# Output and query projections of tiles 1 to 3: low halves one piece ahead, rows behind them, eight more gathered rows

## What is computed

```python
h = rms_norm(x, norm_mix)
q, k, v, u_g, v_g = split(h @ w_in)              # 2048 x 5120
y = concat(rms_norm(stick_breaking(q, k, v)), rms_norm(gmlp(u_g, v_g)))
x = x + y @ w_out                                # the output projection
h2 = rms_norm(x, norm_ffn)
# product-key retrieval, 8 heads x 16 experts of 16384 for each token
s = rms_norm(h2 @ peer_w_query) . sub_keys       # the query projection
idx, gate = top16(s)
act = gelu(einsum('tkd,td->tk', peer_u[idx], h2)) * gate
x = x + einsum('tk,tkd->td', act, peer_v[idx])
```

## Time and profile before

| | us |
|---|---|
| median of 3 runs | 2888.29 |
| lowest and highest | 2881.99, 2889.8 |
| the profiled execution | 2884.2 |
| its span, first to last instruction | 2882.5 |

### The profile page before, as it was taken

The page is one execution under the profiler, slowest core; times in us unless marked ns, Lnnn a source line. Parts: engine busy times, 40 slices in busy tenths (PEclk is TensorE's granted clock), DMA queues, the critical chain, the costliest instruction groups (busy, mean ns, idle before and its releaser), DMA issues.

```text
span 2882.5 us, 43296 instructions
## 1 busy us (share of the span) xinstructions
PE 2769.8 (96%) x17757; PEld 2612.8 (91%) x17757; DVE 2156.8 (75%) x2920; ACT 1256.1 (44%) x1692; POOL 1485.8 (52%) x657
## 2 busy tenths in 40 slices
PE   8899999988999999999999999998999999999998
PEld 6687778866788999999999999998999999999998
DVE  6856897767587778889997677776676777777786
ACT  7656632347424333337775333333333333333332
POOL 0100253322232348872223788887867776767762
PEclk9999999999999999999999999999999999999999
DMA  9747678974697969998999999999999999999996
GB/s 362 297 154 273 242 265 344 341 268 156 252 347 289 359 255 338 339 347 346 361 363 372 379 367 382 375 373 336 359 370 358 385 363 378 377 384 361 384 344 229
DMA packets 188846, 949.47 MB, mean 329 GB/s; under 512 B 17712, under 2 KB 77152, under 8 KB 78912
## 3 DMA queue, kind: packets, MB, share of 16 engines
q1 hardware_dynamic: 116064, 485.54, 45.1%
q0 software_dynamic: 60848, 440.59, 39.2%
q10 hardware_dynamic: 11808, 21.70, 2.1%
HBM read 906.46 MB, written 41.22 MB: 329 GB/s over the span
## 4 chain that ended last, share of the span: by engine, by line
PE 73%; DMA 9%; DVE 9%; ACT 5%; POOL 2%; issue 2%; SPq 0%; ACTq 0%; DVEq 0%; POOLq 0%
PE ps L1847 9%; PE ps L2147 9%; PE ps L2145 9%; PE ps L2146 9%; PE ps L2214 8%; PE ps L2216 8%; PE ps L2215 8%; PE ps L2130 5%; PE ps L1834 3%; DVE ring_lo L1188 3%; DMA rows<-peer_u_rows,idx_far 2%; PE ps L2188 2%; DMA g_in<-gelu_scratch 2%; POOL ring_lo L658 2%; DVE rows L1461 2%; ACT ring_hi L744 2%
## 5 line engine op out<-in xcount | busy, mean ns | idle before, releaser
L658 POOL TENSOR_TENSOR ring_lo<-ring_raw,ring_hi 128x2048 fp32r<-128x2048 f32 x203 | 942.2, 4642 | 527.7 <-ACT ring_hi L744 525.6
L744 ACT ACTIVATE ring_hi<-ring_raw 128x2048 fp32r<-128x2048 f32 x396 | 754.7, 1917 | 664.8 <-DMA ring_raw<-peer_u 233.5
L2214 PE MATMUL ps<-a_hi,ring_hi 128*128 128x304 f32 x2048 | 624.0, 305 | 19.9 <-POOL ring_lo L658 13.8
L2145 PE MATMUL ps<-bT_hi,ring_hi 128*128 128x304 f32 x2048 | 622.7, 304 | 9.8 <-POOL ring_lo L658 8.3
L2216 PE MATMUL ps<-a_hi,ring_lo 128*128 128x304 f32 x2048 | 620.0, 303 | 0.0
L2147 PE MATMUL ps<-bT_hi,ring_lo 128*128 128x304 f32 x2048 | 617.8, 302 | 0.0
L2215 PE MATMUL ps<-a_lo,ring_hi 128*128 128x304 f32 x2048 | 617.0, 301 | 0.0
L2146 PE MATMUL ps<-bT_lo,ring_hi 128*128 128x304 f32 x2048 | 615.7, 301 | 0.0
L1188 DVE TENSOR_TENSOR ring_lo<-ring_raw,ring_hi 128x2048 fp32r<-128x2048 f32 x197 | 460.6, 2355 | 129.8 <-ACT ring_hi L744 129.5
L695 POOL DMA_INDIRECT rows<-peer_u_rows,idx_far x128 | 206.0, 1609 | 452.8 <-DVE z_far L1461 398.0
L2214 PEld LDWEIGHTS ps<-a_hi,ring_hi 128*128 128x128 f32 x2048 | 386.2, 189 | 25.2 <-issue 17.9
(11 more groups left out here) (328 smaller groups left out, 3759.8 us busy)
## 6 DMA issues: line engine op xcount, KB each, us to landing
ring_raw<-peer_u SPq DMA_DIRECT2D x128, 1024.0 KB
ring_raw<-peer_v SPq DMA_DIRECT2D x128, 1024.0 KB
ring_raw<-w_in SPq DMA_DIRECT2D x80, 1024.0 KB
ring_raw<-w_out SPq DMA_DIRECT2D x32, 1024.0 KB
ring_raw<-w_query SPq DMA_DIRECT2D x32, 1024.0 KB
g_quad<-gates_scratch SPq DMA_DIRECT2D x32, 640.0 KB
gelu_scratch<-ahead ACTq DMA_DIRECT2D x72, 152.0 KB
g_in<-gelu_scratch SPq DMA_DIRECT2D x72, 152.0 KB
```

The source lines that it names most:

```text
L658: pool.tensor_tensor(ring_lo[s][:], ring_raw[s][:], ring_hi[s][:].bitcast(F32), ALU.subtract)\
L744: act.activation(ring_hi[place(n)][:], ring_raw[place(n)][:], ACT.Copy).then_inc(hi_ok[SLOT[n]], 1)
L2145: pe.matmul(dst, hi[:, e], bT_hi[:, k, 0:NEAR], start=(k == 0), stop=False)
L2214: pe.matmul(dst, hi[:, col], a_hi[:, par, e, :], start=(e == 0), stop=False)
```

## The change

In the output projection VectorE no longer goes to the low half of piece n+2 before the rows of piece n; it stays at n+1. In the query projection it goes to n+1 instead of n+2. The rows of n follow behind. `ROWS_AT` is changed there: in the output projection the pieces with n % 4 == 3 (115, 119, 123) get two rows instead of one (piece 126 keeps one, 127 none); in the query projection n = 128, 131, 134, 137 and 140 get three instead of two (142 and 143 keep none). That is 62 rows instead of 54 in the two stages. Pieces 144 to 283 keep their counts, with the rows' indices shifted by eight, and pieces 284 to 395 share 139 rows instead of 147.

```diff
@@ -147,7 +147,7 @@
     for n in range(OUT_B, AHEAD - 1):
-        ROWS_AT[n] = 0 if n == QUERY_B - 1 else 1 if n == QUERY_B - 2 or n % 4 == 3 and n < QUERY_B else 2
+        ROWS_AT[n] = 0 if n == QUERY_B - 1 else 1 if n == QUERY_B - 2 else 3 if n >= QUERY_B and n % 3 == 2 else 2
     ROWS_AT[AHEAD - 2] = 0
@@ -1594,7 +1594,6 @@
                     for t in range(TB):
                         add_x1((n - OUT_B) // 4 - 1, t)
-                lo_upto(min(n + 2, QUERY_B))
                 rows_step(ROWS_AT[n])
@@ -1614,7 +1613,7 @@
                 if n > QUERY_B and n % 4 == 0:
                     add_squares((n - QUERY_B) // 4 - 1)
-                lo_upto(min(n + 2, AHEAD - 1))
+                lo_upto(min(n + 1, AHEAD - 1))
                 if n == QUERY_B + 1:
```

## The result

The changed kernel takes 2897.16 us (median, 2879.16 to 2913.27), the kernel before in the same comparison 2881.89 (2873.72 to 2893.0): ratio 1.006, 95% interval 1.0045 to 1.0075. It is slower by 0.6%; I had forecast 2885.3 us and no difference. The profiled execution is 2907.5 us long (span 2905.8), 10 us above its median; before's was 2884.2, so this pair of profiles shows more than the medians do (23.3 against 15.3 us).

What follows compares the result with a forecast made beforehand. TensorE, busy 2769.8 of 2882.5 us, was taken to bound the kernel. Terms -3.0 + 0 + 1.2 - 1.2 + 0 made -3.0 us, from the 2888.3 us median to 2885.3 us, range 2876 to 2897.

Steps and rivals of the forecast that it cites:

- What bounds the kernel: Whole kernel: TensorE busy 2769.8 of 2882.5 us; inside the two projections nothing to win, only to lose.
- The sign that I had named for a wrong Part 2 or 3: TensorE waiting more than 4 us for VectorE's low halves between 754 and 1043 us.
- Part 2: Output projection, three more rows: gathers at 8.5 us per buffer stay balanced, 0 us; +2 at 9.5, +4.5 at 10.
- Part 1: Output projection's tail: low halves one ahead free VectorE at 873.9 instead of 878.3 us; -3.0 us, bounds -3.1 and -0.7.
- Part 3: Query projection, low halves one ahead and five more rows: TensorE waits once, for low half 133, +1.2 us.
- (a): Rival: gathers become the limit in both projections, from 9.5 us per buffer on; 2901 us, chance 0.14.
- Part 4: Behind piece 284, eight rows fewer: a few late loads' idle time is won, -1.2 us, bounds -8.9 and +3.
- The store stall: GpSimd's wait storing the first tile's result, then TensorE's 6.63 us: not removed, change 0, bounds -4 and +4.
- (b): Rival: late stalls vanish, the 8.9 us behind 2095 and the tail's 3.0; 2876 us, chance 0.14.
- The sum: All terms: -3.0 + 0 + 1.2 - 1.2 + 0 = -3.0 us, 2885.3 us on the median; chance 0.60.

Runs made afterwards that it cites:

- the experiment with this part alone: Kernel before with only the output projection's new order and three more rows, late doubled rows moved too; query projection as before: 2883.89 us, 1.0003.
- the changed kernel's second profile: The changed kernel, unedited, run again beside the one with all late doubled rows at pieces with (n-284) % 4 == 0: 2892.12 us, 1.0027 against the kernel before.
- the profile with all landings: Changed kernel with all 27 late doubled rows at pieces with (n-284) % 4 == 0, its second run: 2897.64 us, 1.0047 against the kernel before.
- This part alone: Kernel before with only the query projection's new order and five more rows, late doubled rows mostly at (n-284) % 4 == 0: 2892.20 us, 1.0047.
- doubles forced to phase 1: Kernel before, 28 of 35 late two-row pieces put at (n-284) % 4 == 1, ahead of VectorE's low half: 2939.91 us, 1.0204; second profiled execution 2924.76 us.

## Why the prediction was wrong

**What bounds the kernel** held: the two projections had nothing to give and something to lose. The sign that I had named for a wrong Part 2 or 3, over 4 us of waits for low halves between 754 and 1043, came: 10.1 us in four.

**Part 1 (-3.0)** was right in its mechanism and too small here. VectorE's first addition came at 877.76, not at 875: VectorE was free at 877.4 instead of 873.9, since rows had waited for gathers, and then it waited 0.33 us more for TensorE, which the stalls of Part 2 had made late. Of the three waits for diagonals one of 0.89 us is left. With the clock, which I had not counted in the tail, it is -5.1 us in both profiles of the changed kernel; kernels with the order alone show -0.2 to -5.1.

**Part 2 (0)** failed as well. It was mis-sized by the gather: I took 8.5 us per buffer, and in this stage the median gather is 10.0 to 10.2 us plus 0.3. At 10 us my own count gives +4.5. TensorE stalled 3.67 us and the sixteen pieces took 6.7 us more, 3.0 of it not counted as waits, at least in part the lower clock behind a stall; in the changed kernel's second profile they took 4.0 us more. The larger gain of Part 1 hid this: together the output projection ended at +0.2 us in the profile, and the experiment with this part alone measured 1.0003. The DMA rate came out at 361 GB/s, as worked out (362), so the bytes were not the error; the time of one gather among them was. The Trainium skill (DMA: Bandwidth & Descriptors, Anatomy of one DMA, SWDGE path) gave 4.4 us by my estimate; no gather of the chain in these two stages is under 8.4, and the shortest of the profile with all landings is 6.5.

**Part 3 (+1.2)** is the step that failed most: the wait of TensorE for the low half of piece 133. The place was right; the size was 6.4 us of wait and 2.2 of slow clock, 8.6 instead of 1.2. This part alone gave 1.0047. Two terms of my count were off. First, the 8.5 us per buffer. The chain shows 9.37, 8.46 and 12.25 us from issue to landing, and the same buffer was issued into at 903.18, 915.15, 926.20 and 941.04: 12.0, 11.1 and 14.8 us apart. At 8.33 us per piece and 2.33 rows to a piece the stage asks for a row in 3.6 us, so 10.7 per three buffers. The ring gives less than that, and the deficit adds up. Lo(132) began at 925.85 and ended at 928.1, my time was 928.9; only the three rows behind it, the third batch, spent it: lo(133) ended at 943.9 where I had 940.7, 3.2 us. Second, the need. I left TensorE's time at 939.5, though my own Part 1 starts it earlier; it stood from 937.57 on. So 3.2 us came from the gathers, 2.0 from the earlier start and 1.2 from my sum: 6.4. A gain ahead of a bottleneck is not carried through it; it comes out as a longer wait.

One steady figure for the gather was the weak point, more than its value. The median in this stage is 9.0 us, 9.3 with the issue, where my count gives about 3 us; the three gathers ahead of this low half took 11.7 to 12.7 us in the profile that shows them and 12.25 for the one in the chain. I had 8.5 us from three single gathers and from the waits. Waits of a kernel that isn't limited by its gathers tell only what the late ones overran. The table of DMA issues of before would have pointed higher:
```profile
rows<-peer_u_rows,idx_far POOLq DMA_INDIRECT x128, 9.3
```
But this median is not of these stages. Only 12 of the 128 gathers have a landing in that trace, all issued between 362 and 546 us, and the same row of the changed kernel says 8.8. It would have been a reason for more than 0.14 on rival (a), not a measurement of the term.

**Part 4 (-1.2)** is not told by the first pair of profiles: 755.4 us against 746.5 there, 743.7 in the changed kernel's second. I had taken the stage for steady, and it is a draw in every execution, from 742 to 755 us over the kernels with no doubles forced to phase 1. The lock is a part of it that my bounds of -8.9 and +3 left out. It is not the whole: below ten long low halves their number does not order the stages (three with 752.5 us, five with 746.5). The 8 rows fewer have no effect that rises out of it. The store stall was as large as before (5.91 us, 6.63), as said. The first tile's down stage was 5.7 us longer in the first pair; it spans 468.8 to 481.3 us over the other kernels, so this is spread as well.

**The rivals.** (a) was the nearest, with 2897 us instead of 2901 and 0.14 of the chance. The gathers are the limit: with half the bytes per gather, or a fourth buffer, the loss is gone. Its condition, 9.5 us per buffer, was met in the output projection (10.3 to 10.5) and by the long gathers in a row of the query projection, not by its median (9.3); and the tail's gain was not gone, as it had said. (b) did not come: fewer rows did not clear the late waits.

**The sum** of the first pair of profiles is -5.1, +6.7 and +8.7 us for Parts 1 to 3, 10.3 us where I had -1.8. That of the parts run alone: 1.0003 (output) and 1.0047 (query) make 1.005. The whole gave 1.006 in the main comparison and 1.0027 in the second. The 8.7 to 9.3 us of the query projection, 0.0030 to 0.0032, lie in both profiles of the changed kernel; why the medians are sometimes further apart stays open. A share from late collisions is possible, and no comparison here showed one.

## What to carry to other kernels

Before a consumer is moved to a shorter lead, work out the rate of the ring behind it: buffers over (issue to landing, plus use), against what the stage asks; at a ratio near one the lead is what hides the late transfers, and order and load must be priced together, not one by one. Take the transfer's duration from the stage itself and with its spread, and ask what several long ones in a row do: here the median was 9.0 us, and three of some 12 us made the stall. Count the clock with every stall: it added 2.2 us to one of 6.4 and some 2 us came back in a tail that lost its waits. And profile a kernel twice before a stage's difference is explained: here one pair of profiles showed 9 us in a stage where the second showed -3.

## What the hardware showed that I had not expected

- A gather's issue on GpSimd takes longer beside VectorE's rows. In after:
```profile
903.18 2.75 POOL L695 DMA_INDIRECT rows<-peer_u_rows,idx_far  x1 [24.92 <-DVE z_far L1461]
906.24 1.91 POOL L695 DMA_INDIRECT rows<-peer_u_rows,idx_far  x1 [0.30 <-issue]
...
922.05 0.94 POOL L695 DMA_INDIRECT rows<-peer_u_rows,idx_far  x1 [1.66 <-DVE z_far L1461]
```
  It is 0.94 us when VectorE has nothing to do (it waited until 923.63), and 1.91 to 2.75 here beside rows that read two SBUF tiles (`rows`, `h_far`). That the rows are the reason was not tested by itself; with half gathers the issues took as long (2.03 us in the mean) and the stall was gone, so it is not what sets the stall.
- Two low halves that start 0.17 us apart on VectorE and GpSimd cost VectorE 6.92 us instead of 2.28, and GpSimd nothing (4.60). It can fall the other way. In the same trace, with VectorE 0.06 us ahead:
```profile
2499.67 2.28 DVE L1188 TENSOR_TENSOR ring_lo<-ring_raw,ring_hi 128x2048 fp32r<-128x2048 f32 x1
2499.73 6.69 POOL L658 TENSOR_TENSOR ring_lo<-ring_raw,ring_hi 128x2048 fp32r<-128x2048 f32 x1 [1.36 <-ACT ring_hi L744]
```
  So below 0.2 us the order of the starts in the trace does not tell who is stretched.
- A collision of the two low halves repeats. With the doubles at phase 1 a run of ten (359 to 395) held in one execution and a run of four in another; in the former the four pieces from one to the next take 27.9 to 31.3 us instead of 26.6. Placement alone, with the same work, moved the median by about 55 us.
- Half the bytes in a stage took the DMA share from 0.90 to 0.70, and a 6 us stall brought the clock to 0.65 of full for 6 us behind it.
